# HGRN in a two-block transformer kernel: one matmul per head and level for both token tiles, gates and decays through PSUM, f's weights first, and the delta rule's additions moved

## The reference, cut to what matters

```
# hgrn2_mixer, per head; q, f_pre, i, g are slices of h @ w_in
sig = sigmoid(f_pre)
f = lb + (1 - lb) * sig
k = (1 - lb) * (1 - sig)
...
S_t = diag(f_t) S_{t-1} + k_t v_t^T,  o_t = S_t^T q_t      # over 256 tokens
o = o * sigmoid(g); o = o * rsqrt(mean(o * o) + eps) * norm_w
# first block, each of two layers: x = layer_norm(alpha * x + branch @ w_out)
```

## Time and profile before

| | |
|---|---|
| median of 3 runs | 2816.14 us (2815.36 to 2817.78) |
| the profiled execution's own time | 2815.98 us |
| its span in the trace | 2814.2 us |
| TensorE busy | 2763.7 us, 98% of the span, 12871 matmuls |
| TensorE weight loads busy | 2299.8 us, 82% |
| VectorE busy | 1290.9 us, 46% |
| ScalarE busy | 1377.8 us, 49% |
| GpSimd busy | 2354.1 us, 84% |
| HGRN stage | about 1740 to 2050 us |
| delta rule's groups | about 950 to 1545 us |

### The profile page before, as it was taken

The page is one execution under the profiler, slowest core; times in us unless marked ns, Lnnn a source line. Parts: engine busy times, 40 slices in busy tenths (PEclk is TensorE's granted clock), DMA queues, the critical chain, the costliest instruction groups (busy, mean ns, idle before and its releaser), DMA issues.

```text
span 2814.2 us, 38959 instructions
## 1 busy us (share of the span) xinstructions
PE 2763.7 (98%) x12871; PEld 2299.8 (82%) x12871; DVE 1290.9 (46%) x2601; ACT 1377.8 (49%) x1837; POOL 2354.1 (84%) x1831
## 2 busy tenths in 40 slices
PE   9999999999999899999999999999999999999998
PEld 7888888888878788888888887888878888888886
DVE  5232234323672554755756465748354233233234
ACT  4444444444444565665654545555445444444444
POOL 8988889888888677776877787888879999999997
PEclk9999999999999999999999999999999999999999
DMA  8555555555565444544545455444555565565554
GB/s 288 192 183 183 190 190 190 188 182 176 173 221 183 135 159 149 171 158 150 174 149 164 151 178 188 157 153 144 193 180 179 188 200 187 188 200 188 197 190 132
DMA packets 284353, 502.67 MB, mean 179 GB/s; under 512 B 18021, under 2 KB 68662, under 8 KB 283190
## 3 DMA queue, kind: packets, MB, share of 16 engines
q1 hardware_dynamic: 275606, 482.55, 52.5%
q10 hardware_dynamic: 8608, 18.24, 1.8%
HBM read 498.61 MB, written 2.12 MB: 178 GB/s over the span
## 4 chain that ended last, share of the span: by engine, by line
POOL 54%; PE 24%; issue 21%; POOLq 1%; DVE 0%; DVEq 0%; ACT 0%
POOL wlo L439 54%; PE acc L495 8%; PE acc L496 8%; PE acc L497 8%; POOLq L437 0%; POOLq L434 0%; DVE x_sb L2400 0%; DVE big L2376 0%; POOLq L439 0%; DVE kv L1848 0%; DVEq L165 0%; ACT small L1464 0%; DVE small L2367 0%; POOL eps_sb L433 0%; POOL ones L431 0%
## 5 line engine op out<-in xcount | busy, mean ns | idle before, releaser
L439 POOL TENSOR_TENSOR wlo<-raw,whi 128x512 fp32r<-128x512 f32 x1824 | 2353.6, 1323 | 443.0 <-ACT whi L1066 427.4
L1066 ACT ACTIVATE whi<-raw 128x1024 fp32r<-128x1024 f32 x910 | 958.3, 1060 | 1044.4 <-PE acc L497 1002.3
L495 PE MATMUL acc<-whi,a_lo 128*128 128x512 f32 x2528 | 1001.5, 396 | 8.8 <-DVE x_sb L1848 4.8
L497 PE MATMUL acc<-whi,a_hi 128*128 128x512 f32 x2528 | 986.3, 390 | 0.0
L496 PE MATMUL acc<-wlo,a_hi 128*128 128x512 f32 x2528 | 985.7, 390 | 0.0
L495 PEld LDWEIGHTS acc<-whi,a_lo 128*128 128x128 f32 x2528 | 476.1, 188 | 110.9 <-issue 11.0
L497 PEld LDWEIGHTS acc<-whi,a_hi 128*128 128x128 f32 x2528 | 475.4, 188 | 100.8
L496 PEld LDWEIGHTS acc<-wlo,a_hi 128*128 128x128 f32 x2528 | 476.1, 188 | 96.9 <-issue 1.4
L495 PE MATMUL acc<-whi,b_lo 128*128 128x512 f32 x928 | 365.7, 394 | 0.0
L497 PE MATMUL acc<-whi,b_hi 128*128 128x512 f32 x928 | 361.4, 389 | 0.0
L496 PE MATMUL acc<-wlo,b_hi 128*128 128x512 f32 x928 | 361.2, 389 | 0.0
(11 more groups left out here) (307 smaller groups left out, 2025.6 us busy)
## 6 DMA issues: line engine op xcount, KB each, us to landing
raw<-in_w_in_ret SPq DMA_DIRECT2D x176, 512.0 KB, 4.4
raw<-in_w_in_gdn SPq DMA_DIRECT2D x176, 512.0 KB, 4.4
raw<-in_w_out SPq DMA_DIRECT2D x160, 512.0 KB, 4.5
raw<-in_w_mlp_in SPq DMA_DIRECT2D x128, 512.0 KB, 4.2
raw<-in_w_mlp_out SPq DMA_DIRECT2D x128, 512.0 KB, 4.5
raw<-in_w_in SPq DMA_DIRECT2D x80, 512.0 KB, 4.6
raw<-in_w_mem_kv SPq DMA_DIRECT2D x63, 512.0 KB, 4.8
cb<-log_decays ACTq DMA_DIRECT2D x6, 512.0 KB, 4.2
```

What stands on the lines that cost most here:

```text
L439: part = pool.tensor_tensor(wlo[q % 4][:, c], raw_half[:, c], whi[q % 4][:, c].bitcast(f32), ALU.subtract)
L495: pe.matmul(dst, l, w_h, start=start and block == 0, stop=False)
L497: mm = pe.matmul(dst, h, w_h, start=False, stop=stop and block == KB - 1)
L1066: act.activation(whi[q % 4][:, :], raw[j][:, (q % 2) * HALF:(q % 2 + 1) * HALF], ACT.Copy).then_inc(hi_ready, 1)
```

## The change

In HGRN:
- Of the weight units f comes first. f is transposed at step -1 and q at step 3 (before: q at -1, f at 1); the diagonal goes from step 5 to 6, the output from 24 to 26, the branch's transposes from 30 to 32, ScalarE's root from 29 to 31 and its high parts from 34 to 36.
- ScalarE writes sigmoid(-f) into two further banks (`ka`, `kb`) and sigmoid(f) over the transposed f, at its step 3 for group 0 and 5 for group 1; VectorE makes f and k out of PSUM; ScalarE's logarithm goes to the banks `ga`, `gb` (step 5, for group 1 step 7), and the scan reads them there; q is copied out at ScalarE's step 7 (group 1: 8).
- ScalarE's exponentials of all levels go to one pair of banks, so each waits for the scaling of the level before (`lev_ready`).
- For the levels 1 to 64, `ks` holds of each head one mixed tile of 128 columns: tile 0's decayed k on left blocks and tile 1's decayed q on right blocks; `qs` the counterparts. One matmul of 128 columns per head serves both tiles. Tile 1's triangle comes out transposed; a new step 24, `hgrn_turn_back`, transposes it (4 transposes), and VectorE copies it to `lw`.
- The scaling takes four VectorE instructions of 256 elements per level in place of two of 512. The memsets of `xi` and `ui` go.

In the delta rule: `adds(n - 4)` stands between `gdn_level_p` and `gdn_level_n`, not behind both.

```diff
-        ["qa", "fa", "d0"] + [f"l{s}" for s in LEVELS[0::2]] + ["o0"],
-        ["qb", "fb", "d1"] + [f"l{s}" for s in LEVELS[1::2]] + ["o1"],
-        ["x", "ba"], ["bb"]]),
+        ["fa", "ga", "d0"] + [f"l{s}" for s in LEVELS[0::2]] + ["o0"],
+        ["fb", "gb", "d1"] + [f"l{s}" for s in LEVELS[1::2]] + ["o1"],
+        ["ka", "qa", "x", "ba"], ["kb", "qb", "tb", "bb"]]),
...
             def hgrn_turn(g, n):
                 pe.wait_ge(wide_taken, 2 * (W_HG + 4 * g + 1 + n))
-                turn_natural("hgrn", (("qa", "qb"), ("fa", "fb"))[n], g, (n0, n1)[n])
+                turn_natural("hgrn", (("fa", "fb"), ("qa", "qb"))[n], g, (n0, n1)[n])
...
                 for hh in range(4):
-                    if n == 7:
-                        mm = pe.matmul(dst[:, hh * P:(hh + 1) * P], ks[:, hh * SEQ:hh * SEQ + P], qs[:, hh * P:(hh + 1) * P],
-                                       start=True, stop=True)
-                        continue
-                    for t in range(TT):
-                        at = (2 * hh + t) * 64
-                        mm = pe.matmul(dst[:, at:at + 64], ks[:, hh * SEQ + t * P:hh * SEQ + (t + 1) * P], qs[:, at:at + 64],
-                                       start=True, stop=True)
+                    c = slice(hh * P, (hh + 1) * P)
+                    left = ks[:, hh * SEQ:hh * SEQ + P] if n == 7 else ks[:, c]
+                    mm = pe.matmul(dst[:, c], left, qs[:, c], start=True, stop=True)
                 mm.then_inc(done, 1)
...
-                if q in (-1, 1):
-                    hgrn_turn(g, (q + 1) // 2)
-                if q == 5:
+                if q in (-1, 3):
+                    hgrn_turn(g, (q + 1) // 4)
+                if q == 6:
                     hgrn_diagonal(g)
...
                 if q == 24:
+                    hgrn_turn_back(g)
+                if q == 26:
                     hgrn_out(g)
-                if q == 30:
+                if q == 32:
...
+                if q == 3 + 2 * g:
+                    for n, step in enumerate(("fa", "fb")):
+                        b, _ = full("hgrn", step, g)
+                        to, c = fill("hgrn", ("ka", "kb")[n], g)
+                        act.wait_ge(emptied[to], c - 1)
+                        act.activation(bank[to][:, :], b[:, :], ACT.Sigmoid, scale=-1.0).then_inc(filled[to], 1)
+                        act.activation(b[:, :], b[:, :], ACT.Sigmoid).then_inc(s["forget_ready"], 1)
...
-                        buf = (sq, br)[n % 2]
-                        act.activation(buf[:, :], buf[:, :], ACT.Exp).then_inc(s["lev_exp"], 1)
+                        if n:
+                            act.wait_ge(s["lev_ready"], 8 * g + n)
...
+                        act.activation(banks[1][:, :], (sq, br)[n % 2][:, :], ACT.Exp).then_inc(s["lev_exp"], 1)
...
                 for n in range(3, 7):
                     gdn_level_p(g, n)
-                    gdn_level_n(g, n)
                     if n >= 4:
                         adds(n - 4)
+                    gdn_level_n(g, n)
                 adds(3)
...
+                mixed = ks[:, 0:COL]
+                tt(part(mixed, 0, 0), part(lw[:, :], 0, 0), half(left, 0), MUL)
+                tt(part(mixed, 0, 1), part(cv[:, :], 1, 1), half(right, 1), MUL)
+                tt(half(qs, 0), part(cv[:, :], 0, 1), half(right, 0), MUL)
+                tt(half(qs, 1), part(lw[:, :], 1, 0), half(left, 1), MUL).then_inc(s["lev_ready"], 1)
```

More of the change, by code:

```diff
@@ L265, in build @@
             "inverse_rms": "the rows' scales",
+            "forget_ready": "half of a group's forget gates",
             "ksc_ready": "forget gates and keys of HGRN",
@@ L923, in hgrn_out @@
                         to, at = dst[:, hh * P:(hh + 1) * P], hh * P
-                        own = dt_[:, (2 * hh + t) * P:(2 * hh + t + 1) * P]
+                        own = lw[:, at:at + P] if t else dt_[:, 2 * hh * P:(2 * hh + 1) * P]
                         if t:
@@ L1622, in hgrn_steps @@
                     wide_out(u + 1, 1, ACT.Copy, tiles(n1), 0)
[L1623 removed]
+                if q == 3 + 2 * g:
[5 more added lines that the diff above has]
+                        act.activation(b[:, :], b[:, :], ACT.Sigmoid).then_inc(s["forget_ready"], 1)
+                if q == 5 + 2 * g:
+                    for n, step in enumerate(("ga", "gb")):
+                        to, c = fill("hgrn", step, g)
+                        act.wait_ge(emptied[to], c - 1)
+                        act.activation(bank[to][:, :], dn[:, n * COL:(n + 1) * COL], ACT.Ln).then_inc(filled[to], 1)
+                if q == 7 + g:
                     for n, step in enumerate(("qa", "qb")):
                         copy_out("hgrn", step, g, cv[:, n * COL:(n + 1) * COL])
[L1626 to L1631 removed]
                 if q == 10:
@@ L1636, in hgrn_steps @@
                 for n in range(8):
-                    if q == (9 if n < 2 else 8 + 2 * n):
+                    if q == (8 + 2 * n if n else 9):
                         act.wait_ge(s["lev_arg"], 8 * g + n + 1)
-                        buf = (sq, br)[n % 2]
-                        act.activation(buf[:, :], buf[:, :], ACT.Exp).then_inc(s["lev_exp"], 1)
-                if q == 29:
+                        if n:
+                            act.wait_ge(s["lev_ready"], 8 * g + n)
+                        else:
+                            for step in ("qa", "qb"):
+                                b, c = fill("hgrn", step, g)
+                                act.wait_ge(emptied[b], c)
+                        act.activation(banks[1][:, :], (sq, br)[n % 2][:, :], ACT.Exp).then_inc(s["lev_exp"], 1)
+                if q == 31:
                     head_roots(GROUPS + g + 1)
-                if q == 34:
+                if q == 36:
                     b_parts("hgrn", g, (U_ATT1 + 7, U_P0 + 2)[g], lambda k: cols[:, C_HW + 4 * g + k:C_HW + 4 * g + k + 1])
@@ L2456, in hgrn_scale, with part, half @@
                     turned("hgrn", "x", g - 1)
-                tt(compact(qs, size), sides(cv, size)[1], compact(buf[:, 0:COL], size), MUL)
-                tt(sides(ks, size)[0], sides(lw, size)[0], compact(buf[:, COL:], size), MUL).then_inc(s["lev_ready"], 1)
+                right, left = banks[1][:, 0:COL], banks[1][:, COL:]
+                if n == 7:
+                    tt(compact(qs, size), sides(cv, size)[1], compact(right, size), MUL)
+                    tt(sides(ks, size)[0], sides(lw, size)[0], compact(left, size), MUL).then_inc(s["lev_ready"], 1)
+                    return
+                def part(buf, t, side):
+                    return by(buf, 4)[:, :, t * P:(t + 1) * P].rearrange("p h (b two c) -> p h b two c", two=2, c=size)[:, :, :, side, :]
+                def half(buf, t):
+                    return by(buf, 4)[:, :, 64 * t:64 * (t + 1)].rearrange("p h (b c) -> p h b c", c=size)
+                mixed = ks[:, 0:COL]
[3 more added lines that the diff above has]
+                tt(half(qs, 1), part(lw[:, :], 1, 0), half(left, 1), MUL).then_inc(s["lev_ready"], 1)
             def hgrn_diagonal(g):
@@ L2473, in hgrn_place @@
                 b, done = full("hgrn", f"l{size}", g)
-                for i in range(8):
-                    at = i * P
-                    to = dt_[:, at:at + P].rearrange("p (n two s) -> p n two s", two=2, s=size)[:, :, 1, :]
-                    mask = level_mask(n).bitcast(u32).rearrange("p (n two s) -> p n two s", two=2, s=size)[:, :, 1, :]
-                    last = dve.copy_predicated(to, mask, compact(b[:, i * 64:(i + 1) * 64], size))
+                mask = level_mask(n).bitcast(u32).rearrange("p (b two c) -> p b two c", two=2, c=size)
+                for hh in range(4):
+                    for t in range(TT):
+                        to = dt_[:, (2 * hh + t) * P:(2 * hh + t + 1) * P].rearrange("p (b two c) -> p b two c", two=2, c=size)
+                        at = hh * P + 64 * t
+                        last = dve.copy_predicated(to[:, :, 1 - t, :], mask[:, :, 1 - t, :], compact(b[:, at:at + 64], size))
                 last.then_inc(done, 1)
@@ L2501, in hgrn_levels @@
                         hgrn_arg(g, n + 2)
+                b, done = full("hgrn", "tb", g)
+                dve.tensor_copy(lw[:, 0:COL], b[:, :]).then_inc(done, 1)
                 hgrn_place(g, 7)
```

56 lines of the change are left out of this document (30 added, 26 removed).

## The result

The changed kernel takes **2793.92 us** (median of 6, 2791.72 to 2795.19), the kernel before in the same job 2816.21 (2815.36 to 2817.78 over 6 runs). The ratio is 0.9918 with an interval of 0.9908 to 0.9928: 0.8% faster. Forecast were 2793.9, in 2787 to 2801. The profiled execution took 2795.12, its span 2793.3, against 2815.98 and 2814.2 before.

What follows compares the result with a forecast made beforehand. TensorE, busy 98% of the span, was taken to bound the kernel through its passes, waits and clock. Gains of 12.5, 8.5, 1.0 and 6.7 less losses of 0.9 and 5.7 made 22.1 us: 2815.98 to 2793.9, range 2787 to 2801.

Steps and rivals of the forecast that it cites:

- Levels: HGRN levels: merged passes of 128 columns save 0.89 us per level, seven levels in two groups, 12.5 us gained.
- price per pass: TensorE's level matmuls: a pass costs 0.112 us with 64 or 128 columns alike.
- Turn back: HGRN: four added transposes per group at 0.112 us each, 0.9 us lost.
- Level 0 with its clock: HGRN level 0: both groups' waits for VectorE's scaling go, with the half clock behind them, 8.5 us gained.
- Diagonals: HGRN diagonal: TensorE's waits for k go, 1.0 us gained.
- Delta rule: Delta rule: TensorE's waits for additions go in groups 1 to 5, 1.34 us each, 6.7 us gained.
- fifth wait: Delta rule: one more wait for additions than the four put down to VectorE; without it 5.4 us gained.
- New wait: Group 1's q transposes in HGRN wait for VectorE to empty k's banks: 4.0 us plus 1.7 of clock, 5.7 lost.
- Sum: Whole kernel: 12.5 - 0.9 + 8.5 + 1.0 + 6.7 - 5.7 = 22.1 us gained.
- rival of VectorE's pace: HGRN levels: four VectorE products at 1.78 us each set the pace, costing 68 us; 2862, slower by 46; 4%.
- point of decision: HGRN levels: VectorE products of about 0.95 us decide whether the change is faster or slower.

Runs made afterwards that it cites:

- two_passes: Changed kernel with each level's matmul of 128 columns split into two of 64; 2807.2 us, ratio 0.9965.
- gdn_back: Changed kernel with the delta rule's additions behind both level steps again, HGRN as changed; 2801.34 us, ratio 0.9943.
- q_turn_5: Changed kernel with group 1's q transposes at TensorE's step 5 instead of 3 and ScalarE's copies at its step 9 instead of 8; 2788.87 us, ratio 0.9900.
- q_first: Changed kernel with q's weight unit ahead of f's again, as before the change, PSUM paths kept; 2789.11 us, ratio 0.9903.
- q_turn_4: Changed kernel with group 1's q transposes at TensorE's step 4 instead of 3, nothing else; 2790.22 us, ratio 0.9904.
- merge_alone: Changed kernel with gates, scans and exponentials back in SBUF and q's unit first; merged levels and moved delta rule additions stay; 2813.65 us, ratio 0.9989.

## Why the prediction was right

- **Levels** (12.5): two_passes gives 13.2 within 4, 12.9 in the trace's HGRN, and the bursts 1.79 against 0.90. The price per pass holds.
- **Turn back** (-0.9): four passes cost 0.46 and 0.45.
- **Level 0 with its clock** (8.5): in the trace before, each late start is 2.55 us and the levels behind it come 1.7 later still; 8.5 for both groups together. After, neither is there. The step was right that the margin is 3 us in group 0, but not by its own terms alone: it gave the four scans 4.5 us, they took 2.42, and VectorE spent the difference waiting for the diagonal's product (idle 1.93 and 0.20). In group 1 the margin was 3 and not 2.
- **Diagonals** (1.0): 0.52 twice, gone.
- **Delta rule** (6.7): gdn_back gives 7.0. In the traces the stretch of the delta rule's groups takes 556.02 us before (988.97 to 1544.99) and 549.29 after (989.81 to 1539.10), 6.7 less. The fifth wait is in it, since the four that the list puts down to VectorE make 5.4.
- **New wait** (-5.7): 3.42 at the start and 1.9 behind it, 5.3; undone in q_turn_5, it gives 5.1, and 5.4 in the trace's HGRN. The forecast chain was right to half a microsecond: ScalarE's sigmoids into PSUM are 0.48 apart and last 0.58 to 0.60, which no row had shown.
- **Sum**: HGRN takes 16.4 us less (374.4 to 358.0), and the terms as measured, 12.5 - 0.9 + 8.5 + 1.0 - 5.3, make 15.8; 0.6 has no place of its own. Ahead of HGRN the changed kernel gains 5.9, which is the delta rule's 6.7 less 0.8 that this execution had lost ahead of those groups. Behind HGRN it loses 1.4 in the longer half clock at the boundary. Together that is the 20.9 between the two profiled executions; the forecast was 22.1.

That the median, 2793.92, meets the forecast of 2793.9 is luck in its last digits: the runs of the changed kernel spread over 3.5 us, and the two profiled executions differ by 1.2 less than was forecast. What the traces bear out is each term, to within half a microsecond.

What the prediction had wrong lies in its rivals and in what it took as given. The rival of VectorE's pace had 68 us with products in SBUF; measured are 10.7, as it priced 256 elements like 512 and GpSimd's gaps weren't in it. Its point of decision, products of 0.95, was too low, as the gaps shorten the arguments too: at 1.15 on average the kernel was still faster than before. And the sum counts the merged levels as a gain of their own. They are a full one only with the decays in PSUM. Merging turns two products of 512 elements into four of 256; beside GpSimd, two start 1.70 apart and take 3.4 us, four start 1.43 apart and take 5.7. The Trainium skill, page "SBUF — State Buffer", section "SBUF: two separate sides", says that whichever engine starts first holds the shared pair for its whole instruction and the other blocks. By that rule the wait goes with the number of instructions and with GpSimd's size, and not with VectorE's elements; the waits of 1.10 and 1.09, 0.55 and 0.54 agree.

The best kernel is one of q_first, q_turn_5 and q_turn_4, 2788.9 to 2790.2; their intervals don't separate them, and each beats both kernels given.

## What to carry to other kernels

Count passes of small fp32 matmuls, not their columns: a merged pass gives back the whole price of the one that it saves, if the engine that feeds it keeps the shorter pace. Beside a busy GpSimd, count VectorE's instructions with two SBUF operands: an edit that splits them in two adds one wait for each new instruction (3.4 us became 5.7 here), and an operand in PSUM takes them out of the turns. When a chain is made shorter, undo the reordering that was made for the long one, and look at which bank it now shares.

## What the runs showed that I had not expected

- The scans, 256 elements, are 0.6 us apart with their input in PSUM (2.42 for four) and up to 1.6 with it in SBUF beside GpSimd (3.3 to 6.5 for four, by how much of the time GpSimd runs): I had taken 4.5 for the price of the scan itself, and half of it was GpSimd's turn.
- VectorE's product of 256 elements: 0.41 us out of PSUM or in a gap of GpSimd, 0.96 beside pieces of 256, 1.51 beside pieces of 512. A scalar operation that reads one tensor in SBUF and writes SBUF is held too: 0.28 alone, 1.39 beside GpSimd.
- GpSimd's subtractions last 774 ns with 256 columns against half of 1316 with 512, about 0.12 us more per piece; part of it can be VectorE's turns.
- Single idles of TensorE of 0.54 to 1.74 us inside HGRN left the granted clock at 1.00. Those of 2.18, 2.38, 2.40 and 2.43 were followed by 3.4 us at 0.50, that of 3.26 by 3.4 us or more in six traces and by none in one, those of 4.9 (merge_alone) by 3.4 in one group and by a stretch of 6.8 in the other. At the boundary to the MLP three idles of 1.2, 1.0 and 0.7 to 0.9 stand within 4 us in every trace of the changed kernel and of the first ten variants, and 0, 3.4 or 6.8 us of half clock go with them. So a price for the clock read from one trace is a likely one, not a sure one.
